# Mixture-of-experts block loop: the loop turned, expert rows added in memory by indirect transfers, part of a product on GpSimd

## The reference, cut to what matters

```python
def moe(h, router_w, router_b, w1, b1, w2, b2):
    logits = (h @ router_w + router_b).astype(jnp.float32)
    top_v, top_i = lax.top_k(logits, TOP_K)
    gates = jax.nn.softmax(top_v, axis=-1).astype(h.dtype)
    ...   # assignments sorted by expert, each expert's rows padded to blocks of 128: dest, row_tok, blk_e
    def expert_block(args):
        xb, e = args
        hid = xb @ w1[e] + b1[e]
        return clamped_swiglu(hid[:, :D_FF_3], hid[:, D_FF_3:]) @ w2[e] + b2[e]
    ys = lax.map(expert_block, (xs, blk_e)).reshape(-1, D)
    contrib = ys[dest] * gate_sorted[:, None]
    return jax.ops.segment_sum(contrib, tok_sorted, num_segments=T)
```

## Time and profile before

| | us |
|---|---|
| median of 3 runs | 3776.75 |
| the profiled execution | 3776.74 |
| its span, first to last instruction | 3774.8 |
| TensorE busy | 3347.7 (89%) |
| VectorE busy | 2305.7 (61%) |
| ScalarE busy | 1548.4 (41%) |
| GpSimd busy | 117.1 (3%) |

### The profile page before, as it was taken

How to read it: one execution, slowest core, us unless ns; L and a number is a source line. 1 busy time by engine, 2 the same in 40 slices (tenths; PEclk the granted TensorE clock), 3 DMA queues, 4 the chain that set the end, 5 groups by cost and what they waited for, 6 DMA issues and landing times. The chain is left out here.

```text
span 3774.8 us, 47052 instructions
## 1 busy us (share of the span) xinstructions
PE 3347.7 (89%) x16502; PEld 2588.1 (69%) x16503; DVE 2305.7 (61%) x2926; ACT 1548.4 (41%) x1933; POOL 117.1 (3%) x113
## 2 busy tenths in 40 slices
PE   7887998999968878899987878879999999999996
PEld 5655886884446567788756655667777777777774
DVE  4375665347422454455444474478888888888885
ACT  1262332010033621100123153357777777777772
POOL 0000000000000000000000000000000000000001
PEclk8888999999979987799988989879999999999996
DMA  5401222232102000122273101279999999999995
GB/s 160 154 24 45 89 100 80 99 89 89 67 27 64 1 1 1 50 100 92 89 290 120 56 9 34 77 313 399 363 357 359 361 352 359 364 355 360 359 346 216
DMA packets 182773, 648.58 MB, mean 172 GB/s; under 512 B 14033, under 2 KB 95825, under 8 KB 126210
## 3 DMA queue, kind: packets, MB, share of 16 engines
q1 hardware_dynamic: 165474, 600.56, 43.6%
q0 software_dynamic: 7056, 25.69, 1.8%
q10 hardware_dynamic: 10128, 20.76, 1.4%
HBM read 612.83 MB, written 36.75 MB: 172 GB/s over the span
## 5 line engine op out<-in xcount | busy, mean ns | idle before, releaser
L488 DVE TENSOR_TENSOR experts_rest<-experts_weights,experts_leading 128x2048 fp32r<-128x2048 f32 x384 | 875.3, 2286 | 109.7 <-ACT experts_leading L2990 109.7
L2990 ACT CAST experts_leading<-experts_weights 128x2048 fp32r<-128x2048 f32 x384 | 716.9, 1907 | 50.7 <-ACT experts_y L2982 22.2
L494 PE MATMUL psum<-experts_leading,experts_xT_leading 128*128 128x512 f32 x1024 | 410.9, 401 | 51.5 <-DVE experts_rest L488 51.5
L496 PE MATMUL psum<-experts_leading,experts_xT_rest 128*128 128x512 f32 x1024 | 406.2, 397 | 0.0
L495 PE MATMUL psum<-experts_rest,experts_xT_leading 128*128 128x512 f32 x1024 | 405.6, 396 | 0.0
L494 PEld LDWEIGHTS psum<-experts_leading,experts_xT_leading 128*128 128x128 f32 x1024 | 194.7, 190 | 107.4 <-DVE experts_rest L488 65.3
L496 PEld LDWEIGHTS psum<-experts_leading,experts_xT_rest 128*128 128x128 f32 x1024 | 194.6, 190 | 46.8
L495 PEld LDWEIGHTS psum<-experts_rest,experts_xT_leading 128*128 128x128 f32 x1024 | 194.6, 190 | 43.8
L494 PE MATMUL psum<-experts_leading,experts_hidden_leading 128*128 128x512 f32 x512 | 210.3, 411 | 0.0
L496 PE MATMUL psum<-experts_leading,experts_hidden_rest 128*128 128x512 f32 x512 | 201.2, 393 | 0.0
L495 PE MATMUL psum<-experts_rest,experts_hidden_leading 128*128 128x512 f32 x512 | 201.1, 393 | 0.0
(11 more groups left out here) (757 smaller groups left out, 6802.4 us busy)
## 6 DMA issues: line engine op xcount, KB each, us to landing
experts_weights<-in_w_up SPq DMA_DIRECT2D x256, 1024.0 KB, 6.8
experts_weights<-in_w_down SPq DMA_DIRECT2D x128, 1024.0 KB, 7.5
ada_unit<-in_w_ada SPq DMA_DIRECT2D x12, 2048.0 KB, 17.7
expert_rows<-experts_y ACTq DMA_DIRECT2D x66, 256.0 KB, 7.2
merge_first<-in_w_merge SPq DMA_DIRECT2D x16, 768.0 KB, 4.4
merge_weights<-in_w_merge SPq DMA_DIRECT2D x16, 768.0 KB, 4.1
ff_up_first<-in_w_up SPq DMA_DIRECT2D x11, 1024.0 KB, 4.8
ff_up_weights<-in_w_up SPq DMA_DIRECT2D x11, 1024.0 KB, 4.7
```

The costliest lines, as they stand in the source:

```text
L488: return dve.tensor_tensor(out, src, leading.bitcast(F32), ALU.subtract)
L494: pe.matmul(out, lh, rh, start=start, stop=False)
L496: return pe.matmul(out, ll, rh, start=False, stop=stop)
L2990: act.copy(leading[h % LEADING], place(ring, h)).then_inc(masked, 1)
```

## The change

Four things. (1) The loop is turned: the masks of halves 0, 1 and 2 of the next block, and the splits of halves 0 and 1, stand at the end of a block's list; the weights' buffer is allocated before `route`, which starts the loads of the first three halves. (2) Results no longer go to `expert_rows`. ScalarE copies them from PSUM scaled by the row's gate (`keep_y`), and GpSimd adds the 128 rows into the token's rows of `sums` by one indirect transfer that accumulates; it waits for it to land before it goes on, since the next block may add to the same rows. `sums` (five pieces of 512 KB) is zeroed at the start of `experts`; `route` computes the gates by row (`gate_of`) and target rows (`target_of`), with 16 more matmuls. (3) `combine` reads the four pieces of `sums` instead of gathering 16. (4) For units 0 and 1 the product of gate and linear part is made by GpSimd in two instructions instead of by one on VectorE. Whether a block is filled is now a comparison of registers.

```diff
@@ experts, block.sync
                 def body(i, s, b):
                     mine, following = expert_at(b), expert_at(b + 1)
                     for h in range(AHEAD, HALVES):
                         sp.wait_ge(consumed, b * HALVES + h + 1)
                         weights.load(k, sp, mine, h, landed[h])
                     for h in range(AHEAD):
                         sp.wait_ge(consumed, (b + 1) * HALVES + h + 1)
                         weights.load(k, sp, following, h, landed[h])
...
+                load_bias(0, expert_at(0))
+                for t in range(TT + 1):
+                    sp.dma_start(sums[t * P:(t + 1) * P, :].rearrange("p (a n) -> p a n", n=HALF),
                                  zero[:, :].unsqueeze(1).broadcast_to([P, D // HALF, HALF])).then_inc(zeroed, 16)
+                blocks(sp, body)
@@ experts, block.gpsimd
+                def body(i, s, b):
+                    gather(1 - s, i + s, b + 1)
+                    for u in range(2):
+                        pool.wait_ge(silued, b * UNITS + u + 3)
+                        pool.wait_ge(clipped, b * UNITS + u + 3)
+                        wait_apart(pool, hid_turned, b * UNITS, passed)
+                        pool.tensor_scalar(silu[:, u, :], silu[:, u, :], SILU_LIMIT, None, ALU.min).then_inc(bounded, 1)
+                        wait_apart(pool, bounded, b * 2 + u + 1, passed)
+                        pool.tensor_tensor(product[:, u, :], silu[:, u, :], lin[:, u, :], ALU.mult).then_inc(timed, 1)
+                    pool.tensor_copy(targets[:, s:s + 1], target_of[:, bass.ds(b, 1)]).then_inc(targeted, 1)
+                    pool.tensor_copy(gate_slots[:, s:s + 1], gate_of[:, bass.ds(b, 1)]).then_inc(gates_kept[s], 1)
+                    wait_apart(pool, targeted, b + 1, passed)
+                    for u in range(2):
+                        wait_apart(pool, y_copied[u], b + 2, passed)
+                    pool.indirect_dma_start(out=sums, out_offset=bass.IndirectOffsetOnAxis(ap=targets[:, s:s + 1], axis=0),
+                                            in_=y[:, :, :].rearrange("p u n -> p (u n)"), in_offset=None, compute_op=ALU.add
+                                            ).then_inc(added, 16)
+                    wait_apart(pool, added, b * 16 + 16, passed)
@@ experts, block.scalar
+                    def keep_y(u):
+                        act.wait_ge(consumed, (b + 1) * HALVES + HALVES - 1 + u)
+                        act.wait_ge(gates_kept[s], i + 1)
+                        act.activation(y[:, u, :], k.bank(2 + u), ACT.Copy, scale=gate_slots[:, s:s + 1]).then_inc(y_copied[u], 1)
...
                     mask(11)
                     mask_hidden(2)
+                    mask(0, b + 1)
                     mask_hidden(3)
+                    mask(1, b + 1)
+                    keep_y(0)
+                    act.wait_ge(bias_landed[1 - s], (i + s) * 16 + 16)
+                    mask(2, b + 1)
+                    keep_y(1)
@@ experts, block.vector
                     def clip(u):
                         dve.wait_ge(consumed, b * HALVES + 2 * u + 2 + HALVES)
+                        dve.wait_ge(timed, b * UNITS + u + 1)
...
+                    split_half(2, b)
+                    split_half(3, b)
                     clip(0)
+                    split_half(4, b)
+                    split_half(5, b)
                     clip(1)
+                    split_half(6, b)
+                    split_half(7, b)
                     clip(2)
+                    split_half(8, b)
                     split_hidden(0)
                     split_hidden(1)
                     multiply_gate(2)
...
+                    split_half(11, b)
+                    split_half(0, b + 1)
                     split_hidden(3)
                     split_x(1 - s, i + s)
+                    split_half(1, b + 1)
@@ combine, block.sync and block.tensor
+                for t in range(TT):
+                    sp.dma_start(acc[:, t, :], sums[t * P:(t + 1) * P, :]).then_inc(loaded[t], 16)
...
-                    pe.wait_ge(weighed, TOP_K * (t + 1))
+                    pe.wait_ge(loaded[t], 16)
```

More of the change, by code:

```diff
@@ L2567, in retire, with route @@
             k.places.remove(place)
-def route(k, inputs, rows, bias_parts, residual, gate, dest, row_of, block_expert, gate_by_expert, x_rows, index, first_gathered):
+def route(k, inputs, rows, bias_parts, residual, row_of, block_expert, gate_by_expert, x_rows, index, first_gathered,
+          weights, gate_of, target_of):
     nc, E, K, B = k.nc, EXPERTS, TOP_K, SLOTS_MAX + 1
@@ L2617, in _ @@
                     sp.dma_start(rows[t * P:(t + 1) * P, :], by_token[:, t, :]).then_inc(rows_stored, 16)
+                sp.wait_ge(known, 1)
+                first = sp.value_load(block_expert[0:1, 0:1], min_val=0, max_val=EXPERTS - 1)
+                for h in range(AHEAD):
+                    weights.load(k, sp, first, h, weights.landed[h])
                 sp.wait_ge(rows_stored, 16 * (TT + 1))
@@ L2797, in experts @@
     with k.stage("experts") as (sb, sem):
[L2798 to L2799 removed]
+        rest = k.over("experts_rest", weights.ring[:, :, :], [P, 6, 2 * WIDE])
         places = [k.over(f"experts_leading{n}", x[:, :, :], [P, 2, WIDE]) for n, x in enumerate((k.h, k.x))]
@@ L2824, in down_half, with rest_half, blocks @@
             return (h - 2 * UNITS) % 2, (h - 2 * UNITS) // 2
-        def place(x, h):
+        def rest_half(h):
             u, part = (h // 2, h % 2) if h < 2 * UNITS else (UNITS + down_half(h)[0], down_half(h)[1])
[L2829 to L2844, removed]
+            return rest[:, u, part * WIDE:(part + 1) * WIDE]
+        def blocks(eng, body):
+            filled = eng.value_load(block_expert[0:1, SLOTS_MAX + 2:SLOTS_MAX + 3], min_val=1, max_val=SLOTS_MAX + 1)
             with eng.Fori(0, (SLOTS_MAX + 1) // 2) as i:
-                block_of(i, 0, (0, 1), lambda: block_of(i, 1, (1,)))
+                with eng.If(2 * i < filled):
+                    body(i, 0, 2 * i)
+                    with eng.If(2 * i + 1 < filled):
+                        body(i, 1, 2 * i + 1)
         with nc.Block() as block:
@@ L2972, in _, with mask @@
             def _(act):
+                def mask(h, b):
+                    act.wait_ge(landed[h], b * 16 + 16)
+                    act.wait_ge(consumed, b * HALVES + h + HALVES - LEADING + 1)
+                    act.copy(leading[h % LEADING], weights.half(h)).then_inc(masked, 1)
                 def keep_x(s, i):
```

255 lines of the change are left out of this document (124 added, 131 removed).

## The result

The changed kernel takes 3979.61 us (median of four executions, 3975.71 to 3988.43) against 3778.98 us of the kernel before (median of four): a ratio of 1.0534, 95% interval 1.0517 to 1.055. It is 5% slower. The forecast, 3888, had the sign, and the time lies 9.6 us above the upper end of the range.

What follows compares the result with a forecast made beforehand. TensorE was held at block starts by VectorE's first split, 51.5 us over 32 blocks. Blocks +115.6, start +4.5, end +0.2 and combine -9.0 gave +111 on 3776.7: 3888 us, range 3720 to 3970, own range 3850 to 3970.

Steps and rivals of the forecast that it cites:

- The least that TensorE allows: Experts' blocks: block 5 without its idle time takes 36.23 us, the least TensorE allows.
- What the turn takes away: Block starts: the turned loop removes idle times of 0.73 and 2.35 us; 57 us less if nothing else were late.
- GpSimd's list becomes the bound: Every block: TensorE waits for product 1 behind GpSimd's add, gather and product 0; stall 5.3 us, block 41.5 us.
- The size of L: GpSimd's add: time from issue to landing, taken as 10 us, with range ends 7.1 and 14.
- The steps on GpSimd: Products 0 and 1: 0.55 + 0.15 + 0.95 us each, with steps waiting for the rest of VectorE's splits.
- The clock: Blocks 1 to 31: granted clock's share kept as before, 5 x 1.55 = 7.8 us; up to 40 only in the range.
- Around the loop: Outside blocks 1 to 31: start +4.5 us, end +0.2, combine -9.0.
- (a): Rival, chance 0.30: GpSimd's chain hides, product 1 stalls TensorE 0 to 1 us, time 3715 to 3747.
- (b): Rival, chance 0.08: turn doesn't remove the stall or a 2 us stall replaces it; 3772 to 3785 us.
- (c): Rival, chance 0.12: GpSimd's add takes 20 us or more, stall 12.6, block 48.8, time 4114 us.
- The own range: Whole kernel: 3850 to 3970 us, from L of 7.1 or 14, a start without loss and a falling clock.

Runs made afterwards that it cites:

- E3: Changed kernel with the wait for the add moved behind the next block's gather and products 0 and 1 back on VectorE: 3715.6 us, ratio 0.9837.
- E6: E3 with the loop of ScalarE and VectorE turned back, masks, splits and y copies at the top of the list: 3758.47 us.
- E1: Changed kernel with the wait for the add moved behind the next block's gather and products: 3753.69 us, ratio 0.9934.
- E2: Changed kernel with products 0 and 1 back on VectorE, the wait for the add left in place: 3865.67 us.
- E4: Changed kernel with the indirect transfer only writing its rows, without the addition: 3973.24 us.
- E5: Changed kernel with VectorE's split 8 waiting until GpSimd's product 1 is done: 3955.89 us.
- E8: E3 with TensorE held ahead of product 0 in each block by 12 chained memsets on GpSimd: 3976.63 us, ratio 1.0524.
- E7: E3 with the sums zeroed in the routing stage from the one row of zeroes: 3784.07 us, ratio 1.001.
- E9: E3 with the sums zeroed in the routing stage from 128 otherwise unused partitions: 3713.55 us, ratio 0.9835.

## Why the prediction was right in sign and too low

**The least that TensorE allows** (36.23 us, read from one block): right, E3 has 36.27.

**What the turn takes away**: right. After has no wait at a block's start, and E6 shows it by itself. Its 42.9 us are less than the 57 that I named as the gain at stake, since the stall in E6 is smaller than it was in before.

**GpSimd's list becomes the bound**: right in place and mechanism, the add, the loop, the gather, product 0, product 1 behind split 8, and the stall in every block. E1 and E2 take its two halves away one by one.

**The size of L**: the first term that failed. I took 10 us between bounds of 7.1 and 14; the median from issue to landing is 12.3. Two small terms came on top: the add is issued at 2.7 us of a block where I had 2.1, and in block 10 it is 2960.9 - 2947.5 = 13.4 us from the issue to GpSimd's next instruction, so going round the loop took 1.1 where I had 0.5. Together they put the landing, as GpSimd sees it, at 16.1, near the 16.6 of my upper bound: with L = 14 the steps gave product 1 at 24.3, and it was done at 24.7. That the upper bound fits so well is partly luck, for L itself was 1.7 less. The price of the addition was about right (2.1 us, E4, where I had 1.6 over the gather's 8.4), but I set it on the wrong base: a store or a gather at 7 to 8.4, where a scatter beside these weights takes 10.2 without any addition. The Trainium skill's fit (DMA: Bandwidth & Descriptors, Anatomy of one DMA — SWDGE), 2.0 us and bytes / 436e3, gives 3.2 us for 512 KB by my estimate. With no weights in flight the plain write takes 3.4 (E4), and the trace agrees; beside the weights it takes 10.2, three times that, so the fit is no price for a loaded stage.

**The steps on GpSimd**: right. Product 0 took 0.86 + 0.18 + 0.73 = 1.8 us (I had 1.65), and the exclusion by split 8 cost 1.4, as E5 shows. (In the sum, 1287.7 is 31 x 41.54; 31 x 41.5 would be 1286.5.)

**The clock**: the step that failed most. I carried the clock's share over from before (7.8 us in all) into the sum, although the forecast itself put an idle time of 5.3 us into every block, more than twice the 2.35 behind which rows of before show the fall. I named it as an addition to the range, up to 40 us at 1.55 per block. It is 2.1 per block in after, 66 us in all, and 2.46 in E8. Had the clock been a term of the sum, at 1.55 per block as in before, the forecast would have been 3928; with L = 14 besides, 3971.

**Around the loop**: start +6.7 for +4.5. End +7.9 for +0.2: the last add is issued at 3923.74 and combine starts 16.8 us later, where I had 9.5 for landing and eight empty iterations. In after these run one behind the other. In E3, where the last wait stands behind the loop, the same stretch is 11.8 us (3655.30 to 3667.07), so I take 5 us of the iterations to have been serial; the two kernels differ in the products too. Combine -10.8 for -9.0.

**The rivals.** (a), the chain hides, fell: the stall is 6 us. Its price was right for another kernel: with the wait moved and the products back, E3 lands at its lower end (3715). (b), nothing gained and nothing lost, fell: the turn does remove the stall (E6), but 6 us came in its place. (c), an add of 20 us, fell. The own range, 3850 to 3970, ended where both of its long terms are taken at the clock cost of before, 1.55 us; the clock took more.

## What to carry to other kernels

A wait for a transfer belongs in front of the instruction that needs it, not behind the one that issues it: here the place of one wait is worth 226 us, and 150 us hang on it even with nothing but a gather behind it. Before an engine with spare time gets work that TensorE waits for, list what it already waits for in each round, and whether the busy engine beside it lets it read. When a forecast puts an idle time into TensorE's stream, the slower clock behind it is a term of the sum, read from the rows of before, not a tail of the range. And where the clock already falls in every round, a us less of idle time need not give a us back (E4, E5).

## What the runs showed of the hardware that I had not expected

- An idle time of TensorE of 5.63 us costs 8.09: behind it the clock is 0.64 for 7 us (E8). Stretches of 1.7 us cost nothing (E1).
- An indirect add of 512 KB lands after 6.1 us with no weights in flight (one transfer) and 12.3 beside a stream of weights; without the addition 3.4 and 10.2 (E4).
- 2.6 MB stored from one partition hold a queue for 52 us of issue and the stage for 72.7; from 128 partitions the issue takes 5.4 (E7, E9).
- A shorter transfer can give nothing: 2.1 us less in E4, of which 0.6 show in TensorE's waits and none in the length of a block, since GpSimd is shut out by VectorE's split and the slower clock takes the rest.
- A shorter idle time can cost more clock: 6.0 us of waits per block and 2.1 in no wait (after), 4.8 and 2.7 (E5).
